# Gate and up products with 512 moving columns into two banks a tile, and group norm's end on GpSimd with the last input tile inside the convolutions

## The reference

```python
proj = h @ w_in                       # 1024 -> 5504 columns
y_a, s = rwkv7(p_r)                   # a scan, then group norm:
#   y = (group_norm(y) * gn_w + gn_b + bonus) * g
y_b = hyena(p_h)                      # two long convolutions by DFT, each followed by a gate
m = (sigmoid(g_a) * (y_a @ w_pa) + sigmoid(g_b) * (y_b @ w_pb)) @ w_o
x = layer_norm(alpha * x + gate1 * m)
# layer 0, dense: 2816 hidden columns
f = (silu(h @ w_gate) * (h @ w_up)) @ w_out
# layer 1, 8 experts of 1408 hidden columns; combine = normalised top 2 of the router
f = sum_e (silu(h @ w_gate[e]) * (h @ w_up[e]) * combine[e]) @ w_out[e]
x = layer_norm(alpha * x + gate2 * f)
```

## Time and profile before

| | |
|---|---|
| Median of 3 runs | 2284.32 us (2281.78 to 2293.54) |
| The profiled execution | 2289.57 us, its span 2287.8 us |
| Mean granted PE clock | 0.921 of full speed |
| PE / weight loads / DVE / ACT / POOL busy | 88% / 75% / 50% / 33% / 5% of the span |
| Dense gate/up pairs | 684 to 800 us |
| Experts | 1497 to 2265 us |

### The profile page before, as it was taken

The page is one execution under the profiler, slowest core; times in us unless marked ns, Lnnn a source line. Parts: engine busy times, 40 slices in busy tenths (PEclk is TensorE's granted clock), DMA queues, the critical chain, the costliest instruction groups (busy, mean ns, idle before and its releaser), DMA issues.

```text
span 2287.8 us, 30938 instructions
## 1 busy us (share of the span) xinstructions
PE 2015.5 (88%) x13189; PEld 1709.5 (75%) x13189; DVE 1135.6 (50%) x1458; ACT 759.8 (33%) x924; POOL 106.6 (5%) x161
## 2 busy tenths in 40 slices
PE   6789998898779997788988878789999999999996
PEld 2766666665669986666765657788988989899895
DVE  1635444336665546544444475544545545455454
ACT  1332222324134433322223332343433434343342
POOL 3011000000020000101001000000000000000000
PEclk9869989899989998779898999799999999999998
DMA  9403323324155553221232322246555555555552
GB/s 288 132 27 112 112 75 112 112 84 124 55 161 186 185 200 93 69 74 57 93 94 93 97 88 86 98 129 194 185 175 174 168 193 173 186 168 183 186 164 83
DMA packets 247417, 301.27 MB, mean 132 GB/s; under 512 B 8427, under 2 KB 224080, under 8 KB 247152
## 3 DMA queue, kind: packets, MB, share of 16 engines
q1 hardware_dynamic: 240112, 286.28, 39.1%
q0 software_dynamic: 4192, 11.28, 1.6%
q10 hardware_dynamic: 2976, 1.73, 0.3%
HBM read 297.69 MB, written 1.57 MB: 131 GB/s over the span
## 4 chain that ended last, share of the span: by engine, by line
PE 78%; DVE 12%; ACT 4%; issue 4%; DMA 1%; ACTq 0%; DVEq 0%; SPq 0%
PE PS L665 13%; PE PS L666 12%; PE PS L667 12%; PE PS L708 6%; PE PS L995 5%; PE PS L996 5%; PE PS L997 5%; PE PS L833 2%; ACT WH L1106 2%; PE PS L830 2%; PE PS L783 2%; DVE WL L1387 2%; PE PS L851 1%; DVE WL L1396 1%; DMA WRING<-in_w_ada 1%
## 5 line engine op out<-in xcount | busy, mean ns | idle before, releaser
L665 PE MATMUL PS<-HTH,WH 128*128 128x256 f32 x2448 | 725.1, 296 | 81.2 <-DVE WL L1396 38.0
L1387 DVE TENSOR_TENSOR WL<-WRING,WH 128x2048 fp32r<-128x2048 f32 (+1 forms) x213 | 460.2, 2162 | 533.2 <-ACT WH L1106 530.8
L666 PE MATMUL PS<-HTL,WH 128*128 128x256 f32 x2448 | 707.2, 289 | 0.0
L667 PE MATMUL PS<-HTH,WL 128*128 128x256 f32 x2448 | 706.5, 289 | 0.0
L1106 ACT ACTIVATE WH<-WRING 128x2048 fp32r<-128x2048 f32 (+1 forms) x213 | 385.9, 1812 | 691.6 <-PE PS L667 443.8
L665 PEld LDWEIGHTS PS<-HTH,WH 128*128 128x128 f32 x2448 | 481.3, 197 | 103.8 <-issue 65.2
L666 PEld LDWEIGHTS PS<-HTL,WH 128*128 128x128 f32 x2448 | 482.2, 197 | 1.2 <-issue 0.5
L667 PEld LDWEIGHTS PS<-HTH,WL 128*128 128x128 f32 x2448 | 481.7, 197 | 0.0
L708 PE MATMUL PS<-WRING,CONDT 128*2 128x256 f32 x768 | 197.7, 391 | 5.7 <-DMA WRING<-in_w_ada 4.6
L995 PE MATMUL PS<-WH,AH 128*128 128x512 f32 x440 | 171.8, 391 | 13.9 <-DVE WL L1387 13.9
L996 PE MATMUL PS<-WH,AL 128*128 128x512 f32 x440 | 171.3, 389 | 0.0
(11 more groups left out here) (319 smaller groups left out, 2179.3 us busy)
## 6 DMA issues: line engine op xcount, KB each, us to landing
WRING<-in_exp_w_in SPq DMA_DIRECT2D x80, 1024.0 KB, 5.4
WRING<-in_w_ada SPq DMA_DIRECT2D x48, 1024.0 KB, 5.2
WRING<-in_w_in SPq DMA_DIRECT2D x42, 1024.0 KB, 5.4
WRING<-in_exp_w_out SPq DMA_DIRECT2D x40, 1024.0 KB, 5.0
WRING<-in_ffn_w_in SPq DMA_DIRECT2D x22, 1024.0 KB, 5.1
WRING<-in_ffn_w_out SPq DMA_DIRECT2D x11, 1024.0 KB, 4.9
WRING<-in_w_o SPq DMA_DIRECT2D x8, 1024.0 KB, 5.0
WRING<-in_exp_w_in SPq DMA_DIRECT2D x16, 512.0 KB, 3.8
```

Source lines behind the costliest of these rows:

```text
L665: mm(out, h[:, kb, c], hi[:, kb, :], start=kb == 0, stop=False)
L666: mm(out, h[:, kb, c], lo[:, kb, :], start=False, stop=False)
L667: last = mm(out, s[:, kb, c], hi[:, kb, :], start=False, stop=kb == k - 1)
L1387: tt(WL[:, m % 2, 0:k * w], WRING[:, n % RING, 0:k * w], WH[:, m % 2, 0:k * w].bitcast(F32), ALU.subtract)\
```

## The change

1. *HT.* HTH and HTL become the two halves of one tensor HT, so that both can be the moving operand of one product.
2. *Pairs.* `pair_product` multiplies a block of WH with both halves at once: 512 columns, 256 for hi x hi and 256 for hi x lo side by side in one bank; lo x hi is added to the first 256. A tile is 16 products of 512 columns and 16 of 256. Each column block has a bank of its own: gate tiles take banks 0 and 1, up tiles banks 2 and 3. The halves are added afterwards: ACT copies the second 256 columns to LOWS, DVE adds the first ones. Silu then reads SBUF, and on ACT it stands between `make_hi(n + 2)` and `make_hi(n + 3)` and waits for DVE's sum.
3. *Router, parameters.* Their products go to bank 4 where banks 2 and 3 are now taken.
4. *Group norm's end.* DVE keeps the reciprocal; seven GpSimd instructions do the rest (`gating`). The bonus has a buffer of its own. YAH and YAL are made in the second convolution.
5. *Order.* The first turn of z stands ahead of the filters' spectra. Input tile 21 is multiplied inside the first convolution, one half ahead of the inverse DFT and one behind it, and ACT and DVE split its successor there.

```diff
-                  ("filter", l, 2), ("gn", l, 3), ("filter", l, 3), rest[2][0], ("gn", l, 4), rest[2][1],
-                  ("turn_z", l)]
+                  ("turn_z", l), ("filter", l, 2), ("gn", l, 3), ("filter", l, 3)]
...
+        HT = sb("HT", [P, 2, KB, TOK], F32R)
+        HTH, HTL = HT[:, 0, :, :], HT[:, 1, :, :]
...
+            def gating(l):
+                pool.wait_ge(ev("gn_rstd"), l + 1)
...
+                steps(pool.tensor_tensor(YT[:, :, :], YT[:, :, :], TMP2[:, :, :], ALU.mult))
+                steps.wait()
+                for b in range(4):
...
+                    steps(pool.tensor_scalar(YT[:, b, :], YT[:, b, :], PT[:, gw:gw + 1], PT[:, gb:gb + 1], ALU.mult, ALU.add))
+                steps.wait()
+                steps(pool.tensor_tensor(YT[:, :, :], YT[:, :, :], BONUS[:, :, :], ALU.add))
+                steps.wait()
+                pool.tensor_tensor(YT[:, :, :], YT[:, :, :], GATE[:, :, :], ALU.mult).then_inc(ev("ya"), 1)
...
+            def pair_product(n):
...
+                for b in range(w // P):
+                    c = slice(b * P, (b + 1) * P)
+                    for kb in range(k):
+                        mm(PS[:, bank_of[n] + b, :], h[:, kb, c], HT[:, :, kb, :], start=kb == 0, stop=False,
+                           skip_group_check=True)
+                        last = mm(PS[:, bank_of[n] + b, 0:TOK], s[:, kb, c], HT[:, 0, kb, :], start=False, stop=kb == k - 1,
+                                  skip_group_check=True)
...
@@ PE, conv
+                if o == 0:
+                    product(number["in", l, 21, 0], HTH, HTL, 0, 2)
                 for g in range(G):
                     pe.wait_ge(ev("spectrum"), 2 * i + g + 1)
...
+                if o == 0:
+                    product(number["in", l, 21, 0], HTH, HTL, 1, 2)
...
@@ ACT, conv
                 if o == 0:
+                    make_hi(number["in", l, 21, 0] + 2)
+                    mix(l, 21)
                     copy_z(l, 1)
                 else:
+                    act.wait_ge(ev("ya"), l + 1)
+                    fn(YAH[:, :, :], YT[:, :, :], ACT.Copy).then_inc(ev("ya_hi"), 1)
...
@@ ACT, pair
                 make_hi(n + 2)
                 act.wait_ge(tile_done, n + 1)
+                fn(LOWS[:, 0, 0:nb, :], PS[:, bank_of[n]:bank_of[n] + nb, TOK:2 * TOK], ACT.Copy).then_inc(ev("low_half"), 1)
+                act.wait_ge(ev("gate_sum"), u + 1)
+                fn(SL[:, u % 2, 0:nb, :], SL[:, u % 2, 0:nb, :], ACT.Silu).then_inc(ev("silu"), 1)
                 make_hi(n + 3)
+                act.wait_ge(tile_done, n + 2)
+                fn(LOWS[:, 1, 0:nb, :], PS[:, bank_of[n + 1]:bank_of[n + 1] + nb, TOK:2 * TOK], ACT.Copy).then_inc(ev("low_half"), 1)
...
                 act.wait_ge(ev("hidden"), u + 1)
...
@@ DVE, gn part 3
+                    dve.reciprocal(TMP2[:, :, :], TMP2[:, :, :]).then_inc(ev("gn_rstd"), 1)
...
@@ DVE, conv, between the spectrum and the skip products
+                if o == 0:
+                    make_lo(number["in", l, 21, 0] + 2)
...
@@ DVE, conv, behind the skip products
+                if o:
+                    dve.wait_ge(ev("ya"), l + 1)
+                    dve.wait_ge(ev("ya_hi"), l + 1)
+                    tt(YAL[:, :, :], YT[:, :, :], YAH[:, :, :].bitcast(F32), ALU.subtract).then_inc(ev("ya_lo"), 1)
...
@@ DVE, pair
                 make_lo(n + 2)
+                dve.wait_ge(ev("low_half"), 2 * u + 1)
+                tt(sl, first(n), LOWS[:, 0, 0:nb, :], ALU.add).then_inc(ev("gate_sum"), 1)
...
+                dve.wait_ge(ev("silu"), u + 1)
                 if l % 2 == 1:
...
+                    steps(tt(sl, sl, cb, ALU.mult))
+                make_lo(n + 3)
+                dve.wait_ge(ev("low_half"), 2 * u + 2)
+                steps(tt(up, first(n + 1), LOWS[:, 1, 0:nb, :], ALU.add))
+                steps.wait()
...
+                tt(sl, sl, up, ALU.mult).then_inc(ev("hidden"), 1)
```

115 lines of the change are left out of this document (53 added, 62 removed).

## The result

The changed kernel takes 2344.3 us (median of 4 runs, 2337.6 to 2347.2) against 2284.5 us for the kernel before (4 runs): a ratio of 1.0249, 95% interval 1.0225 to 1.0273. It is slower, as forecast, but by 60 us where 27 were forecast, and outside the range. The profiled execution took 2343.03 us, its span 2341.2 us, against 2289.57 and 2287.8.

A forecast was written before the change was run, and what follows sets the result against it. The prediction took PE to bound the feed-forward part before the change and an ACT-DVE chain after it. Dense 6, experts 15, table load 2 and mixer 4 made +27 us on 2284.32, so 2311 us, range 2289 to 2330.

The forecast's parts named there:

- The chain of nine links: Feed-forward pairs: ACT and DVE alternate in a chain of 11.81 us a pair, longer than PE's new pair of 11.06.
- The upper bound I had named, 0.05 a crossing: Feed-forward chain: 0.05 us on each of six links between engines, 0.3 us a pair, 11 us either way over 38 pairs.
- The dense layer's +6: Dense layer: the longer chain delays the down tiles, the third starting at 141.7 instead of 135.9; a loss of 6 us.
- The table load: Feed-forward: Silu's table load comes behind the wait, 1.3 us on the dense chain once; 2 us in the first expert.
- PE's tile: Pairs: a full tile takes PE 5.53 us instead of 5.68, with long products 0.2271 us and short ones 0.1183 apart.
- the rival in which these products run slower: Pairs: long products miss 0.227 us as their moving operand lies in two pieces; 18 us per 0.01 beyond cover; chance 0.03.
- The experts' 1.9 us: Expert stage: the chain binds after one pair and costs 1.9 us an expert, 15 for eight.
- PE's wait would be named WL, near 0.75 us: Dense pairs, a sign of being right: PE waits before every second tile for DVE's WL, near 0.75 us.
- The mixer's +2 a layer: Mixer: -1.0 us before contention and 3 of contention make +2 a layer, +4 for both (from -2 to +12).
- The contention of 3: Mixer: GpSimd and DVE hold each other up in the spectrum's instructions, 3 us a layer, at most 7.7.
- I take the first, since PE idles for only 1.4 us: Mixer, first DFT product to spectrum: 1.76 us at the full clock taken, not 3.38 at the half one.
- GpSimd holds DVE up wholly: Mixer rival: +7 or more a layer, with the feed-forward at +27, 2322 to 2335 us; chance 0.14.

The follow-up runs named there:

- e6: Changed kernel with VectorE's subtraction of tile 21's successor moved behind the first convolution's skip products; ratio 1.0213 to the kernel before.
- e12: Changed kernel with GpSimd starting group norm's end only when VectorE has finished the first convolution's spectrum; ratio 1.0177 to the kernel before.
- e11: Changed kernel with Silu behind rounding n+3, that tile's subtraction ahead of the Silu wait and combine product, copy into AH unmoved; ratio 1.0280 to the kernel before.
- e1: Kernel before with the new pairs (long products, halves added afterwards, HT, router banks) and the old mixer; ratio 1.0197 to the kernel before.
- e2: Changed kernel's mixer (group norm's end on GpSimd, tile 21 inside the convolution) with the old pairs; ratio 1.0035 to the kernel before.

## Why the prediction was wrong

- *The chain of nine links* was right in kind and order. It was sized 11.81 and measures 11.99: 0.83 instead of 0.73 from the up sum to the product, which waits for the sum to be written, 0.71 instead of 0.66 from the copy into AH to the next rounding, and 0.54 instead of 0.50 from Silu to the rounding. The upper bound I had named, 0.05 a crossing, covered that.
- *The dense layer's +6* met the measured +5.8, partly by luck. The chain's 0.18 us more made 1.8 over ten pairs. The table load, put on the chain with 1.3 us, cost 0.2, since it runs while ACT waits. And the first gate tile was done 1.0 us sooner than in the kernel before, since the clock rose sooner there; with the same start, as in e6 and e12, it is +6.7.
- *PE's tile* of 5.53 us is 5.65. I had taken 0.2271 from the earlier trace rows, another product with another moving operand, and gave 0.03 to the rival in which these products run slower. In the dense layer it made no difference, as the chain bound. Among the experts PE does bind for a part of the period, and there the saving was counted and not there, some 0.12 us for each such tile.
- *The experts' 1.9 us*, with 2 for the table load 17 in all, measured 42.2, and this is the step that made the prediction wrong. Two things failed in it. First, I had asked how long PE waits and never what it does after the wait: the sum has no term for the clock. Behind two waits of 1.8 and 2.8 us an expert it falls to 1.2 GHz more often than not, where it fell three times in all before. That is 15 of the 25 us missing. Second, the chain itself was too short: with the full clock an expert takes 3.5 us more than before and not 1.9. In the expert shown, the rounding of pair 1 starts 18.2 us behind PE's first product and not 17.7; pairs 1 to 3 take 11.96 each instead of 11.81; and from the rounding of the first half tile to the next pair's it is 9.4 us and not 8.0, since the second half tile's rounding waits for PE to finish the last full up tile. The 2 us for the table load did not come; the first expert takes 2.8 more. Without the clock's 15 us the time would have been some 2329 us (estimate), at the upper end of the range.
- *PE's wait would be named WL, near 0.75 us.* It is 0.69 a pair, and named DVEq: the banks, one instruction further down the same chain. It did not matter to the sum, but it misled the next forecast, that of e11. PE's busy share in the dense pairs is 96%, not below 95.
- *The mixer's +2 a layer* measures +2.8 to the second spectrum and 0.8 behind it (65.7 us from there to the GBC copy in e1, 66.5 in e2): 3.6, or 7 for both, against 4, and e2's 8 agrees. (The kernel before has 64.2 behind it in layer 0; e1 with the same mixer has 65.7, so I do not count this 1.5.) The spectrum starts 7.0 us behind the reciprocal's start and not 9.1, 2 better than forecast. The contention of 3 measures 3.4; its upper bound should have been +13 for both layers by its own terms, not +12. The step that failed is "I take the first, since PE idles for only 1.4 us": not there, but behind the contention PE idles 4.7 us and in the turn 6.3, and at half the clock the inverse DFT, half a tile, the turn and the second DFT take about 3.4 us longer. The subtraction ahead of the skip products was rightly seen to take back the early start; e6 gives it 4.3 us.
- *The rivals.* "GpSimd holds DVE up wholly" (0.14) was the nearest in size and not the cause: the mixer gave 4 us more than its share, the experts 25.
